# One expert layer, two gate rows to four: fetching the experts' gate and up weights in 4 KB runs, in pairs of raw buffers

## What is computed

```python
for e in range(N_EXPERTS):                      # 32 experts, D_MODEL 1024, EXPERT_FF 256
    hid = jax.nn.silu(jnp.matmul(h, w_gate[e])) * jnp.matmul(h, w_up[e])
    out = out + jnp.matmul(hid, w_down[e]) * combine[:, e:e + 1]
```

## Time and profile before

| | |
|---|---|
| median of 3 runs | 2043.73 us (2040.54 to 2049.68) |
| profiled execution, its own time | 2044.95 us |
| its span in the trace | 2043.3 us |
| TensorE busy, share of span | 96% |
| VectorE / ScalarE / GpSimd busy | 57% / 51% / 15% |
| granted TensorE clock, mean | 0.994 |

### The profile page before, as it was taken

How to read it: one execution, slowest core, us unless ns; L and a number is a source line. 1 busy time by engine, 2 the same in 40 slices (tenths; PEclk the granted TensorE clock), 3 DMA queues, 4 the chain that set the end, 5 groups by cost and what they waited for, 6 DMA issues and landing times.

```text
span 2043.3 us, 27995 instructions
## 1 busy us (share of the span) xinstructions
PE 1957.5 (96%) x10551; PEld 1687.6 (83%) x10551; DVE 1172.9 (57%) x2306; ACT 1037.0 (51%) x1705; POOL 312.9 (15%) x420
## 2 busy tenths in 40 slices
PE   7999999999999998999999999999999989999998
PEld 7977877777777776789999999999788777877887
DVE  3345388554999998744444444444444536736772
ACT  4654534444788787654444444444443555345341
POOL 2601232011000001201120112011010002402310
PEclk9999999999999999999999999999999999999999
DMA  4411221146899999412222222222244312122121
GB/s 147 143 44 40 73 78 58 42 149 230 295 368 362 359 372 350 144 47 75 73 70 70 67 74 70 70 69 93 75 159 134 124 42 65 39 62 67 59 103 42
DMA packets 178017, 255.58 MB, mean 125 GB/s; under 512 B 13565, under 2 KB 92234, under 8 KB 177882
## 3 DMA queue, kind: packets, MB, share of 16 engines
q1 hardware_dynamic: 168832, 221.33, 33.0%
q0 software_dynamic: 8784, 31.92, 4.2%
q10 hardware_dynamic: 266, 0.52, 0.1%
HBM read 239.57 MB, written 14.16 MB: 124 GB/s over the span
## 4 chain that ended last, share of the span: by engine, by line
PE 78%; DVE 11%; ACT 5%; DMA 3%; issue 2%; POOL 0%; SPq 0%; ACTq 0%; DVEq 0%
PE pb L2405 51%; PE pb L2433 6%; PE pb L2776 5%; DVE wlo L1574 3%; PE pb L2799 3%; PE pb L3000 2%; PE pb L2919 2%; ACT whi L951 2%; PE pb L2489 2%; PE pb L2502 2%; PE pb L2908 2%; DMA wraw<-w_down 1%; DMA wraw<-w_up 1%; DVE arena L2179 1%; PE pb L3019 1%
## 5 line engine op out<-in xcount | busy, mean ns | idle before, releaser
L2405 PE MATMUL pb<-whi,AT_hi 128*128 128x512 f32 (+4 forms) x1992 | 777.5, 390 | 13.5 <-DVE arena L2179 5.4
L1574 DVE TENSOR_TENSOR wlo<-wraw,whi 128x1024 fp32r<-128x1024 f32 (+4 forms) x430 | 490.3, 1150 | 518.0 <-ACT whi L951 513.6
L2405 PE MATMUL pb<-whi,AT_lo 128*128 128x512 f32 (+4 forms) x1992 | 726.7, 365 | 0.0
L2405 PE MATMUL pb<-wlo,AT_hi 128*128 128x512 f32 (+4 forms) x1992 | 725.1, 364 | 0.0
L951 ACT ACTIVATE whi<-wraw 128x1024 fp32r<-128x1024 f32 (+4 forms) x446 | 440.7, 993 | 381.6 <-PE pb L2405 319.7
L2405 PEld LDWEIGHTS pb<-whi,AT_hi 128*128 128x128 f32 x1992 | 376.7, 189 | 65.0 <-issue 17.3
L2405 PEld LDWEIGHTS pb<-wlo,AT_hi 128*128 128x128 f32 x1992 | 377.1, 189 | 44.3 <-issue 6.5
L2405 PEld LDWEIGHTS pb<-whi,AT_lo 128*128 128x128 f32 x1992 | 375.4, 188 | 45.0
L2433 PE MATMUL pb<-arena 128*128 128x128 f32 (+1 forms) x1180 | 177.4, 278 | 27.3 <-ACT arena L987 6.2
L2433 PEld LDWEIGHTS pb<-arena 128*128 128x128 f32 (+1 forms) x1180 | 143.9, 145 | 62.9 <-ACT arena L1051 9.1
L2776 PE MATMUL pb<-whi,AT_hi 128*128 128x512 f32 x256 | 103.6, 405 | 1.5 <-DVE AT_lo L1920 1.5
(11 more groups left out here) (315 smaller groups left out, 2375.1 us busy)
## 6 DMA issues: line engine op xcount, KB each, us to landing
wraw<-w_in_a SPq DMA_DIRECT2D x288, 128.0 KB
wraw<-w_gate SPq DMA_DIRECT2D x128, 256.0 KB
wraw<-w_up SPq DMA_DIRECT2D x128, 256.0 KB
wraw<-w_down SPq DMA_DIRECT2D x58, 512.0 KB
wraw<-w_in_b SPq DMA_DIRECT2D x40, 512.0 KB
wraw<-w_in SPq DMA_DIRECT2D x28, 512.0 KB
wraw<-w_mem_kv SPq DMA_DIRECT2D x16, 512.0 KB
wraw<-w_in_a SPq DMA_DIRECT2D x16, 512.0 KB
```

Of the source, the lines that this page charges most:

```text
L1574: dve.tensor_tensor(w_slot(wlo, p, p % SPL), raw_slot(p), w_slot(whi, p, p % SPL).bitcast(F32), ALU.subtract).then_inc(lo_done[p % SPL], 1)
L2405: mm = pe.matmul(ACC[bank][:, 0:n], a, b, start=kc == 0 and q == 0, stop=i == c["count"] - 1 and kk == per - 1 and q == 2)
```

## The change

Three things are changed together.

1. **Runs of 4 KB.** A partition now takes four neighbouring rows of gate (one quad, 4 KB that lie together) in one raw buffer, and the same four rows of up in the next one. Each raw buffer is filled by one DMA of 512 KB. The number of gate-and-up DMAs falls from 256 to 128, the bytes stay.
2. **Pairs.** The split pieces in `whi` and `wlo` look as before (two rows of gate beside the same two of up), so that TensorE's code hardly changes. Each of the two split pieces of a pair reads half of both raw buffers (`raw_halves`). Therefore a split waits for both buffers to have landed, and a buffer may be filled again only when both splits are done (`both_of`). The row that a contraction chunk stands for changes too, so the gathered rows are read with a stride of 4 elements instead of 2 (`x_col`), and the norm's gains are loaded to match.
3. **Other held pieces.** A pair has to lie at an even place of the ring. The six held pieces are now both down pieces of experts 4, 14 and 24.

```diff
+        HELD_EXPERTS = (4, 14, 24)
-        by_pair = lambda w: w.rearrange("e (q p j) f -> e q p (j f)", p=P, j=2)
-        gate_rows, up_rows = by_pair(A["w_gate"][0]), by_pair(A["w_up"][0])
+        by_four = lambda w: w.rearrange("e (q p j) f -> e q p (j f)", p=P, j=4)
+        gate_rows, up_rows = by_four(A["w_gate"][0]), by_four(A["w_up"][0])
             if kind == "gu":
-                pieces.append(([(512 * i, 512, w[ex, q].unsqueeze(1)) for i, w in enumerate((gate_rows, up_rows))], 1, PIECE))
+                pieces.append(([(0, PIECE, (gate_rows, up_rows)[q % 2][ex, q // 2].unsqueeze(1))], 1, PIECE))
...
-        NHELD = 6
-        HELD = [P_MOE + 14 + 24 * i for i in range(NHELD)]
+        HELD = [piece_of["dn", n, b] for n in HELD_EXPERTS for b in range(2)]
+        NHELD = len(HELD)
...
+        GU = {piece_of["gu", n, q]: q % 2 for n in range(NEXP) for q in range(4)}
+        assert all(ring_at(p) % 2 == GU[p] and p not in HELD for p in GU)
+
+        def both_of(p):
+
+            return [p - GU[p], p - GU[p] + 1] if p in GU else [p]
+
+        def raw_halves(p):
+
+            if p not in GU:
+                return raw_slot(p)
+            a = ring_at(p - GU[p]) % RAW
+            return wraw[:, a:a + 2, 512 * GU[p]:512 * GU[p] + 512]
...
                 if p not in HELD and ring_at(p) >= RAW:
-                    before = RING[ring_at(p) - RAW]
-                    sp.wait_ge(lo_done[before % SPL], before // SPL + 1)
+                    for before in both_of(RING[ring_at(p) - RAW]):
+                        sp.wait_ge(lo_done[before % SPL], before // SPL + 1)
...
-                act.wait_ge(*raw_loaded(p))
+                for b in both_of(p):
+                    act.wait_ge(*raw_loaded(b))
                 if p >= SPL:
                     act.wait_ge(piece_used, p - SPL + 1)
-                act.activation(w_slot(whi, p, p % SPL), raw_slot(p), ACT.Copy).then_inc(hi_done, 1)
+                act.activation(split_slot(whi, p), raw_halves(p), ACT.Copy).then_inc(hi_done, 1)
...
-                transposes("moe", 2 * g + i, [x_col[g % 2][:, 2 * i + k // 2, k % 2, :] for k in range(4)])
+                transposes("moe", 2 * g + i, [x_col[g % 2][:, i, k, :] for k in range(4)])
```

More of the change, by code:

```diff
@@ L311, in raw_slot, with split_slot @@
             return wraw[:, ring_at(p) % RAW, 0:slot_cols(p)]
+        GU = {piece_of["gu", n, q]: q % 2 for n in range(NEXP) for q in range(4)}
[7 more added lines that the diff above has]
+            return wraw[:, a:a + 2, 512 * GU[p]:512 * GU[p] + 512]
+        def split_slot(buf, p):
+            w = w_slot(buf, p, p % SPL)
+            return w.rearrange("p (w c) -> p w c", w=2) if p in GU else w
         def raw_loaded(p):
@@ L516, in build @@
         x_row = [big[:, D * i:D * i + D] for i in range(2)]
-        x_col = [x.rearrange("s (q c j) -> s q j c", c=P, j=2) for x in x_row]
+        x_col = [x.rearrange("s (q c j) -> s q j c", c=P, j=4) for x in x_row]
         row_pair = lambda a, r: a[:, r:r + 2, :].rearrange("p a b -> p (a b)").rearrange("p (k s) -> p k s", k=KD)
@@ L782, in _ @@
             with nc.allow_non_contiguous_dma(reason="gains as columns"):
-                pool.dma_start(g_moe.rearrange("p (q j) -> p q j", j=2),
-                               A["norm_ffn_g"][0].rearrange("(q p j) -> p q j", p=P, j=2)).then_inc(S("g_moe_in"), 16)
+                pool.dma_start(g_moe.rearrange("p (q j) -> p q j", j=4),
+                               A["norm_ffn_g"][0].rearrange("(q p j) -> p q j", p=P, j=4)).then_inc(S("g_moe_in"), 16)
             link(pool.memset(qaT[96:P], 0.0))
@@ L1573, in feed @@
                 dve.wait_ge(hi_done, p + 1)
-                dve.tensor_tensor(w_slot(wlo, p, p % SPL), raw_slot(p), w_slot(whi, p, p % SPL).bitcast(F32),
+                dve.tensor_tensor(split_slot(wlo, p), raw_halves(p), split_slot(whi, p).bitcast(F32),
                                   ALU.subtract).then_inc(lo_done[p % SPL], 1)
```

## The result

| | before | changed |
|---|---|---|
| median | 2046.36 us (2040.54 to 2049.68, 4 runs) | 2071.76 us (2068.53 to 2073.95, 4 runs) |
| ratio | | 1.012, 95% interval 1.0096 to 1.0145 |
| span of the profiled execution | 2043.3 us | 2069.5 us |

The change makes the kernel 1.2% slower, some 25 us. The forecast was 2040.2 us with a range of 2034 to 2053.

A forecast was written before the change was run, and what follows sets the result against it. The prediction took TensorE as the bound, held up in the expert stage by weight supply, with 5.7 us to gain. A 4.7 us gain less 1.2 for pair coupling took 2043.7 to 2040.2 us, range 2034 to 2053.

The forecast's parts named there:

- the floor of 251.5 us for 28 experts: Expert stage: seven groups of four experts at the fast group's 35.93 us, against 257.2 us before.
- The time allowed for a pair: Expert stage, from SyncE's refill to ScalarE's need: 6.4 us for half a pair before, 4.9 for both halves after.
- the first rival: Expert stage: pairs starve the ring of raw buffers, making the kernel slower, 2059 us at b = 1.0; 18 in 100.
- the pair coupling: Expert stage: pairs that land late, meeting a gather of a group's rows, cost 1.2 us in all.
- the held pieces: Expert stage: same 8.7 us of DMA, now in three lumps; part of the stage's forecast gain of 4.7 us.
- the load of a pair: Weight DMA in the expert stage: fixed time plus data for 1.05 MB, together 4.3 to 5.6 us.
- the price without cover: Expert stage: if lateness is not hidden, each late pair costs TensorE 0.7 us, 20 us over 28 experts.
- the 1.8 us hidden behind a late split: VectorE's low part ends at 593.6, TensorE wants it about 595.4, so 1.8 us of lateness stay hidden.
- this very loop: A pair's load plus its splits in the expert stage closes in 7.8 to 9.1 us, mostly under an expert's 8.98.
- The rival's formula: Expert stage pace of 8.74 + b us per expert, b being how long the queue runs dry after each expert.
- The packets: Weights' queue: 4 KB runs save 0 to 27 us of DMA time, middle 14, or 0.43 us per expert.
- At nothing: Items priced at zero: splits' own cost, extra ScalarE and SyncE waits in idle time, fewer DMAs freeing SyncE.

The follow-up runs named there:

- experiment 11: Kernel before, no pairs and 2 KB runs, with all 64 down pieces in a ring of their own made of the six held buffers; 2041.58 us, ratio 0.9971.
- experiment 2: Experiment 1 plus both pair waits (split and refill), with the old layout and 2 KB runs; 2083.57 us, ratio 1.0167 to the kernel before.
- experiment 1: Kernel before with only the held pieces changed, to both down pieces of experts 4, 14 and 24; 2051.2 us, ratio 1.002.
- experiment 9: Changed kernel with all 64 down pieces in a ring of their own, made of the six held buffers; 2045.88 us, again 2042.82; ratios 0.9986, 0.9981 to before.
- experiment 10: Experiment 9 with runs of 2 KB, still one DMA per gate or up buffer; 2041.86 us, ratio 0.997 to the kernel before.
- experiment 3: Kernel before with each gate-and-up piece fetched by one DMA of 4 KB runs, no pairs, products not the reference's; 2050.03 us, ratio 1.0013.
- experiments 4 and 5: Experiment 2 with only SyncE's refill wait, 2063.85 us, ratio 1.0072; or only ScalarE's wait for both buffers, 2063.61 us, ratio 1.0075 (both to before).
- experiments 7 and 8: Changed kernel with each gate or up load as two DMAs of 512 columns, 2088.55 us; or one DMA of 2 KB runs, 2074.71 us.

## Why the prediction was wrong

**What holds.** The bound and its size were right: the floor of 251.5 us for 28 experts, read from the fast group, is 252.5 in experiment 11, where six of the seven groups take the 35.9 us of that fast group. The most that a better supply can give was put at 5.7 us; experiment 11 gave 4.7 in the stage and 5.9 by its ratio, whose interval is wide. The time allowed for a pair, 6.4 us before and 4.9 after, was the right quantity, and the first rival named the mechanism that came true. Its signs came too: ScalarE waits 56.8 us for the DMA, over the 30 named, and the DMA share is 0.93 and 0.91 in the two stretches.

**The step that failed is the 1.2 us taken for the pair coupling.** It measured 32.4 us with the old loads (experiment 2 over 1; 30 by the ratios), and with the change's two DMAs per pair about 20.6 (changed kernel over experiment 1). With the 4 us of the held pieces that is the whole loss of 25. Two parts of the working led there.

First, the load of a pair was put at 4.3 to 5.6 us, from transfers that land alone. The two rows taken for that, 3.1 and 4.1 us, are not loads at all but GpSimd's stores to memory (`out`, `x_mid`). The same list has loads of 512 KB, four of each kind, which took twice as long:

```profile
arena<-x SPq DMA_DIRECT2D x4, 512.0 KB, 7.2
...
arena<-x_mid POOLq DMA_DIRECT2D x4, 512.0 KB, 9.1
```

And the chain before, in the same working, had 6.39 to 7.77 us for loads within the stage. A pair does not land alone: it stands in the queue behind the other pair or the down pieces, and the two waits of the chain shown above are 7.19 and 4.96 us from the second issue, 0.44 after the first. In the chain from 560 to 800 us there are 16 such links, from 4.44 to 7.46 us. With the 0.44 to the first issue of a pair, from which the 4.9 allowed are counted, all but one exceed it. (The chain shows only loads that somebody waited for.) How often it would happen, once or twice per expert, was forecast well: ScalarE waited 35 times for an up buffer. But it was 1.5 us each time on average, up to 3.6, not up to 0.7. The 20 us that the text names as the price without cover is close to the 20.6 by luck, since it is worked out with 0.7.

Second, the 1.8 us hidden behind a late split were counted as free each time. They are hidden from TensorE, but not from the refill: a split that starts late ends late, and so do the refill and the next landing. Lateness is not used up once per expert, it goes round. The changed kernel's chain shows such a turn:

```profile
696.38 5.65 DMA wraw<-w_up
702.10 1.07 ACT whi L972
703.19 2.37 DVE wlo L1595 x2
705.62 0.35 SPq L732
706.07 5.01 DMA wraw<-w_up
```

From issue to issue it takes 9.69 us, more than the 8.98 of an expert, and TensorE has no part in it. The prediction had this very loop at 7.8 to 9.1 us, with its load of 4.3 to 5.6. Experiments 9 and 10 confirm it from the other side: with the ring deep enough the same pairs cost nothing that can be told.

**The rival's formula** gave the pace as 8.74 + b, and the measured 9.94 us would make b 1.2 instead of 1.0. That is no test of it, since b was measured nowhere and the 8.74 holds the gains of packets and held pieces that did not come. Its weight of 18 in 100 was too low: the range of the load straddled the time allowed, and I let "mostly under" decide for the other side.

**The packets.** The middle of 0 and 27 us was taken, 14 us. Experiment 3 shows 1.8% per KB, 3.4 us, and no time: with 4 KB in all of its rows SyncE's queue costs 43.6 ns per KB, not the 40.0 of GpSimd's. The estimate that I made of the fixed cost of a packet by the Trainium skill ("DMA: Bandwidth & Descriptors", section "Why small descriptors are slow"), 2% and some 4 us, agrees with the row of experiment 3. Splitting one queue's mean by the price of another queue was the mistake; why the other is cheaper is not shown. The cost per KB moves with how full the pipe is kept: 44.8 in the changed kernel (0.849 x 3840 / 72.70, first row below), more than before in spite of the long runs, and 43.3 with runs of 2 KB in the deep ring (0.948 x 3840 / 84.15, experiment 10, second row). With runs of 4 KB in the deep ring it is 42.3 (0.922 x 3840 / 83.61, experiment 9, third row), so there too the run is worth some 2% per KB and no time.

```profile
q1 hardware_dynamic: 19964, 72.70, 84.9%
```

```profile
q1 hardware_dynamic: 36742, 84.15, 94.8%
```

```profile
q1 hardware_dynamic: 23436, 83.61, 92.2%
```

**The held pieces.** I read the last two groups' 75.87 us as 37.93 each and blamed the missing held piece for both. The start between them in TensorE's timeline before says otherwise:

```profile
755.38 0.47 PE L2799 MATMUL pb<-whi,AT_hi 128*128 128x512 f32 x1 [0.35 <-DVE AT_lo L2018]
```

The two take 36.3 and 39.5 us, and the first of them, which has no held piece by the prediction's count, is no slower than the groups that have one (35.9 to 36.7). So the missing piece does not explain which group is slow, and 3.6 of the 5.7 us above the floor are in the last one alone. In experiment 11, where the supply is no limit, the last group is also the longest, 37.1 us against 35.9, so 1.2 us of what I gave to the DMA there has another cause, which no run here looked for. Where the held pieces lie does count, but the other way than forecast: the sum had them as part of a gain of 4.7 us, and experiment 1 costs 4.

**At nothing** was wrong for the extra waits of ScalarE and SyncE, which do not lie in idle time but are what experiments 4 and 5 price. The fewer DMAs, put at nothing as well, may be worth 0.6% once the ring starves (experiments 7 and 8). It was right for the splits' own cost: reading two runs of 512 on the raw side instead of one of 1024 changed the time of neither engine. The groups of the splits in the changed kernel from 560 to 800 us (count, busy time, mean ns of one, idle time before them), as in the earlier trace rows:

```profile
L1595 DVE TENSOR_TENSOR wlo<-wraw,whi 128x1024 fp32r<-128x1024 f32 x139 | 165.1, 1220 | 35.0 <-ACT whi L972 28.6 <-issue 5.8
L972 ACT ACTIVATE whi<-wraw 128x1024 fp32r<-128x1024 f32 x139 | 142.1, 1056 | 66.9 <-DMA wraw<-w_up 47.4 <-PE pb L2797 8.1 <-issue 5.9
```

A split takes 1220 and 1056 ns, within 10 ns of before.

## What to carry to other kernels

When a change makes two buffers of a ring into one unit, count the ring in units: six buffers in pairs are three, and the time from refill to need must cover the queue in front of the load, not a load that lands alone, and least of all a store. Read that queueing time from the chain (6.4 to 7.8 us here, before the change), and take the distance of refill to need as the budget. If three engines and the DMA are all near full, look first at whether the DMA engines ever run dry; depth for the ring, here by giving one kind of piece buffers of its own, gave 0.3% where longer packets gave nothing.

## What the runs showed of the hardware that was not expected

- A load of 64 partitions is dear here. Cutting 512 KB into two DMAs of 64 partitions, with the runs still at 4 KB, raised the queue's cost from 44.8 to 62.2 ns per KB; cutting it into two of 512 columns over all 128 partitions only to 46.7 (0.821 x 3840 / 67.45, row below).

```profile
q1 hardware_dynamic: 31369, 67.45, 82.1%
```

- The DMA share was 0.99 before, in the fast stretch and in the slow, and 1.01 and 1.02 in experiment 11, where 380 GB/s are moved instead of 364 and 352, with the same loads of the same size. A share of 0.99 thus did not mean that no more could be moved: the engines' time per KB fell too, from 44.4 to 43.3 ns (0.950 x 3840 / 84.19).
